# Which engine subtracts which weight remainders in an expert loop: gate+up halves on VectorE, down weights on GpSimd

## What is computed

```python
def expert_step(acc, inp):
    wg, wu, wd, c = inp
    hid = jax.nn.silu(t @ wg) * (t @ wu)
    return acc + c[:, None].astype(t.dtype) * (hid @ wd), None
```

## Time and profile before

| What | Value |
|---|---|
| median of 3 runs | 521.92 us (520.37 to 522.99) |
| profiled execution, its own time | 524.47 us |
| its span, first to last instruction | 522.7 us |
| PE busy | 458.4 us (88%) |
| DVE busy | 351.4 us (67%) |
| ACT busy | 257.7 us (49%) |
| POOL busy | 155.1 us (30%) |
| L574, remainders of a on POOL, 128 x 1024 | 32 in all, about 2.6 us each in the page's mean |
| L1288, remainders of c on DVE, 128 x 1024 | 32, mean 1630 ns |
| L1282, remainders of b on DVE, 128 x 1024 | 30, mean about 1210 ns |

### The profile page before, as it was taken

The page is one execution under the profiler, slowest core; times in us unless marked ns, Lnnn a source line. Parts: engine busy times, 40 slices in busy tenths (PEclk is TensorE's granted clock), DMA queues, the critical chain, the costliest instruction groups (busy, mean ns, idle before and its releaser), DMA issues.

```text
span 522.7 us, 7094 instructions
## 1 busy us (share of the span) xinstructions
PE 458.4 (88%) x2819; PEld 396.8 (76%) x2819; DVE 351.4 (67%) x506; ACT 257.7 (49%) x382; POOL 155.1 (30%) x104
## 2 busy tenths in 40 slices
PE   2799999999999899995999985899999999999500
PEld 2378888899898899995999975777877877877400
DVE  3414688755677969797733457368788788788357
ACT  5615283424453242226211361278888888887412
POOL 3510000000000000202100042477887887885100
PEclk9799999999999899998999997899999999999955
DMA  7532222240202222060496044269999999982175
GB/s 285 223 141 66 96 81 81 80 144 19 81 0 81 82 81 81 0 242 1 128 399 242 5 164 158 84 234 351 341 359 378 360 369 366 356 307 112 29 281 222
DMA packets 20496, 92.96 MB, mean 178 GB/s; under 512 B 6204, under 2 KB 6248, under 8 KB 12008
## 3 DMA queue, kind: packets, MB, share of 16 engines
q1 hardware_dynamic: 15784, 81.94, 42.4%
q0 software_dynamic: 4096, 8.40, 4.9%
q10 hardware_dynamic: 576, 2.10, 1.0%
HBM read 87.18 MB, written 11.53 MB: 189 GB/s over the span
## 4 chain that ended last, share of the span: by engine, by line
PE 63%; DVE 18%; ACT 8%; DMA 4%; issue 3%; POOL 1%; SPq 0%; POOLq 0%; DVEq 0%
PE bank L1385 44%; DVE actl L1288 6%; ACT acth L836 3%; ACT acth L820 2%; PE bank L1638 2%; PE bank L1640 2%; PE bank L1639 2%; PE bank L1626 2%; DMA X<-in_x_dram 2%; DVE arena L1342 1%; PE bank L1528 1%; PE bank L1544 1%; DMA arena<-pairs_dram 1%; PE bank L1666 1%; PE bank L1392 1%
## 5 line engine op out<-in xcount | busy, mean ns | idle before, releaser
L1385 PE MATMUL bank<-wh,acth 128*128 128x256 f32 x320 | 92.9, 290 | 1.4 <-DVE arena L951 1.4
L1385 PE MATMUL bank<-wh,actl 128*128 128x256 f32 x320 | 91.9, 287 | 0.0
L1385 PE MATMUL bank<-wl,acth 128*128 128x256 f32 x320 | 91.8, 287 | 0.0
L574 POOL TENSOR_TENSOR wl<-raw,wh 128x1024 fp32r<-128x1024 f32 x22 | 57.0, 2611 | 70.9 <-ACT wh L809 70.9
L537 POOL TENSOR_TENSOR arena<-arena,bc 128x1024 f32<-128x1024 f32 x2 | 5.3, 2670 | 206.6 <-DVE arena L963 206.6
L1385 PEld LDWEIGHTS bank<-wh,acth 128*128 128x128 f32 x320 | 63.1, 197 | 1.6 <-issue 1.6
L1385 PEld LDWEIGHTS bank<-wl,acth 128*128 128x128 f32 x320 | 62.8, 196 | 0.0
L1385 PEld LDWEIGHTS bank<-wh,actl 128*128 128x128 f32 x320 | 62.7, 196 | 0.0
L1288 DVE TENSOR_TENSOR actl<-arena,acth 128x1024 fp32r<-128x1024 f32 x32 | 52.1, 1630 | 2.7 <-ACT acth L820 1.0
L1638 PE MATMUL bank<-wh,acth 128*128 128x512 f32 x128 | 53.4, 417 | 0.5 <-DVE actl L1274 0.3
L1385 PE MATMUL bank<-acth,wh 128*128 128x512 f32 x128 | 50.5, 394 | 0.0
(11 more groups left out here) (287 smaller groups left out, 998.5 us busy)
## 6 DMA issues: line engine op xcount, KB each, us to landing
raw<-in_w_units_dram SPq DMA_DIRECT2D x18, 1024.0 KB, 4.8
raw<-in_w_gate_up_dram SPq DMA_DIRECT2D x17, 1024.0 KB, 11.3
arena<-in_w_down_dram SPq DMA_DIRECT2D x16, 1024.0 KB, 13.9
arena<-in_w_gate_up_dram SPq DMA_DIRECT2D x15, 1024.0 KB, 13.0
arena<-pairs_dram SPq DMA_DIRECT2D x8, 512.0 KB, 7.3
X<-in_x_dram SPq DMA_DIRECT2D x4, 512.0 KB, 6.0
arena<-in_x_dram SPq DMA_DIRECT2D x1, 2048.0 KB, 9.7
h_dram<-X ACTq DMA_DIRECT2D x4, 512.0 KB, 3.5
```

What stands on the lines that cost most here:

```text
L574: gp.tensor_tensor(wl[:, 0, c], raw_a[b][:, c], wh[:, 0, c].bitcast(F32), ALU.subtract).then_inc(wla_ok, 1)
L1385: ins = te.matmul(acc_ap, a, b, start=(j == 0), stop=(j == n - 1))
```

## The change

The three subtractions keep their sizes, types and number. DVE takes a and b, POOL takes c. On DVE the a half stands behind b and ahead of the evacuation of the result, and for expert 1 it stands ahead of the loop. On POOL c of expert e+1 stands behind the gather and ahead of the scatter of e. Ahead of the loop POOL subtracts b and then c of expert 0 (a and then b before), and DVE subtracts a of expert 0 after the tables (c before).

```diff
-            def split_a(step, e):
+            def split_c(step, e):
                 b = e % WSETS
                 for h in range(2):
                     c = slice(h * UNIT // 2, (h + 1) * UNIT // 2)
-                    pool.wait_ge(wha_ok, step * 2 + (h + 1))
-                    gp.tensor_tensor(wl[:, 0, c], raw_a[b][:, c], wh[:, 0, c].bitcast(F32),
-                                     ALU.subtract).then_inc(wla_ok, 1)
+                    pool.wait_ge(whc_ok, step * 2 + (h + 1))
+                    gp.tensor_tensor(wcl[:, c], raw_c[b][:, c], wch[:, c].bitcast(F32),
+                                     ALU.subtract).then_inc(wlc_ok, 1)
...
                 if not first_round:
-                    split_a(base, 0)
-                split_a(base + 1, 1)
+                    split_c(base, 0)
                 for e in range(NE):
-                    if e + 2 < NE:
-                        split_a(base + e + 2, e + 2)
                     if e + HGB < NE:
                         gather(base, e + HGB, first_round)
+                    if e + 1 < NE:
+                        split_c(base + e + 1, e + 1)
                     scatter(r, base, e)
 
-            split_a(0, 0)
             for h in range(2):
...
+            split_c(0, 0)
...
-            def split_c(step, e, h):
-                c = slice(h * UNIT // 2, (h + 1) * UNIT // 2)
-                dve.wait_ge(whc_ok, step * 2 + (h + 1))
-                ve.tensor_tensor(wcl[:, c], raw_c[e % WSETS][:, c], wch[:, c].bitcast(F32),
-                                 ALU.subtract).then_inc(wlc_ok, 1)
+            def split_a(step, e):
+                for h in range(2):
+                    c = slice(h * UNIT // 2, (h + 1) * UNIT // 2)
+                    dve.wait_ge(wha_ok, step * 2 + (h + 1))
+                    ve.tensor_tensor(wl[:, 0, c], raw_a[e % WSETS][:, c], wh[:, 0, c].bitcast(F32),
+                                     ALU.subtract).then_inc(wla_ok, 1)
 
             def dve_expert(r, base, e, first_round):
                 step, b = base + e, e % 2
                 if e + 1 < NE:
                     rest_tokens(step + 1, 1 - b)
-                if e:
-                    split_c(step, e, 0)
                 dve.wait_ge(sil_ok, step + 1)
                 ve.tensor_tensor(hid, bank[b][:, FE:2 * FE], sil, ALU.mult).then_inc(hid_ok, 1)
-                if e:
-                    split_c(step, e, 1)
                 dve.wait_ge(hh_ok, step + 1)
                 ve.tensor_tensor(hidl[:, :], bank[4][:, 0:FE], hidh[:, :].bitcast(F32), ALU.subtract).then_inc(hl_ok, 1)
                 if e + 1 < NE:
                     split_b(step + 1, e + 1)
+                if e + 2 < NE:
+                    split_a(step + 2, e + 2)
...
-                split_c(base, 0, 0)
-                split_c(base, 0, 1)
+                split_a(base, 0)
                 if not first_round:
                     split_b(base, 0)
                 rest_tokens(base, 0)
+                split_a(base + 1, 1)
```

## The result

The changed kernel takes 538.36 us (median of 4, 537.32 to 539.66), the one before 522.33 in the same comparison. The ratio is 1.0307 with a 95% interval of 1.0278 to 1.0337: **16.0 us slower**, where 13.2 were forecast. The profiled execution took 539.66 us, and its span is 537.9. T stands for the end of the down product of the expert before.

A forecast was written before the change was run, and what follows sets the result against it. PE's own work was taken to bound the loop, with a stall of about 0.35 us an expert on top. Loop 10.0, last expert 0.8, expert 0 0.6 and routing 1.8 made +13.2: 535.1 us at the median, range 530 to 548.

The forecast's parts named there:

- What bounds the kernel now: Expert loop before the change: PE's own work, plus hid queued behind VectorE's held c half, about 0.35 us an expert.
- The loop: Experts 1 to 14: the down product waits about 0.9 for GpSimd's c; period 10.46 us, +10.0 us in all.
- Covers: In the loop, VectorE's late token remainders cost PE no wait or 0.1 to 0.5, hidden under its wait for c.
- the rival in which they starve: Loop: gather and scatter wait out VectorE's four subtractions, delaying GpSimd's next pair; +12.5, 547.6 us, chance 0.14.
- The routing: Ahead of the loop: VectorE's small operation L1218 meets GpSimd's fourth half; +1.8 us, bounds 0 and 2.3.
- The early loads: Expert 3's a and b loads leave with the gathers and may delay the second one; bounds 0 and +0.7, taken as 0.
- VectorE's order: Expert 0: VectorE subtracts a of expert 1 ahead of expert 1's token remainders, delaying PE's first a half; +0.6 us.
- The last expert: Its down product waits for GpSimd's c, starts at T+5.99 and ends at T+9.06 instead of T+8.24; +0.8 us.

The follow-up runs named there:

- the old order: Changed kernel, but ahead of the loop GpSimd again subtracts a and b of expert 0 and VectorE c; 533.68 us, ratio to before 1.0254.
- half of c: Changed kernel, but GpSimd's pair subtracts only the first 512 columns of each half of c; 518.77 us, ratio to before 0.9939.
- shared c: Changed kernel, but in the loop GpSimd subtracts the first half of c and VectorE the second; 530.49 us, ratio to before 1.0141.
- down product by halves: Changed kernel, but PE runs both output banks with c's first half, then its second, waiting for each half alone; 529.54 us, ratio to before 1.0140.
- 8 and 16 matmuls: Changed kernel plus 8 or 16 matmuls into a free bank in the last expert's idle stretch of PE; 537.98 us with 8, 539.0 with 16.

## Why the prediction was right, and where it was short

- **What bounds the kernel now: right.** The stall of `hid` behind the held c half was put at 0.35 us an expert and 4 to 5 us in all. With half of a left out on GpSimd 14 experts took 131.69 instead of 136.43.
- **The loop: right.** Forecast 10.46 an expert from ACT's start of c, the pair of 4.75 and a down product of 3.07; measured 10.49. The order of the causes is shown as well: with the pair short the period is 9.41, and with the pair off PE's path VectorE's chain sets 9.89, a little less than the 10.05 that follows from the chain's 6.8.
- **Covers: right.** The token remainders were said to come up to 0.5 late under PE's wait for c. With that cover gone PE waited for them up to 0.7 (its weight loads up to 1.1), in every second expert. Gather and scatter got in between VectorE's subtractions and were done at T+11.6 (11.7 forecast), so the rival in which they starve did not come.
- **The routing: right.** +1.7 against +1.8. L1217, the fourth small operation with two inputs, took 2.26 where its like had 0.17, and it went away with the old order.
- **The early loads: the term of the sum that was mis-sized.** I bounded it at 0.7 from the landing time of a gather in the loop, 9.7, and took 0 because the loads begin with the gathers. They begin behind the second gather's issue, and it landed 10.75 after it in the changed kernel, 1.05 later than the bound had it. PE also asked for it at 337.21 and not at 337.85, so it waited 2.4, and it lost clock. The price is 2.0 in that profile (23.57 less 21.56). VectorE's order took 0.4 beside it (0.6 forecast). The bound was a median under load, and what counted was one transfer with 2 MB issued right behind it.
- **The last expert: +2.3 in the profile against +0.8.** The start of its down product, T+5.96, was forecast at T+5.99: the wait was right. The down product then ran 4.59 instead of 3.07 at a clock that had fallen. The clock was not in the sum, but the table above has the same fall without the change's longer wait, so these 1.5 are not shown to come from the change. The mean effect of the change on it is open, and by the medians it is small.

So the 2.8 us between forecast and result are the second gather for the most part: 2.0 by the profiles, 2.9 by the medians, 1.3 by the ratios. The loop added another 0.5, with 10.49 an expert for the 10.46 of the forecast.

## What to carry to other kernels

Before handing a step to the slower engine, ask how much lead its operand has. a could be rounded and subtracted two experts ahead, and its pair on GpSimd cost 0.34 us an expert, and that only through VectorE's wait. c can't be touched before the last down product is over, so on GpSimd all that its pair takes beyond some 3.8 us (an estimate, from the prediction's sum) stands on the path. Add up what two engines need of a resource that they take in turns: here GpSimd's pair (4.75) and VectorE's four (4.7) fill 9.45 of a period of 9.41 to 9.8. Both assignments of whole units that were measured, a or c on GpSimd, paid a wait somewhere (b on GpSimd was not run). What gained was a finer cut, half of c, with a consumer that takes operands as they come; the finer cut alone did not. And a step that releases a landing buffer also times a load: moving it can put 2 MB in front of a transfer that someone waits for.

## What the runs showed that I had not expected

- The first gathers landed 5.2 us after issue (median of four) where no load left beside them, and the second one 10.75 after its issue where two 1 MB loads were issued 0.9 and 1.3 us behind it. The same order ahead of the loop stood in six profiled kernels (changed, half of c, shared c, down product by halves, 8 and 16 matmuls), and expert 0 ended 22.7 to 26.2 after the first gather's start in them: the delay is not a fixed price.
- Profiles with the same idle stretch of 1.83 us in PE had a granted clock of 0.62 and of 1.00 in the down product behind it. So had two with 1.03 us (0.63 and 1.00).
- VectorE's row of the second c half begins at 400.58, GpSimd's at 400.77 (above), and GpSimd still went first: VectorE's took 3.64 for 1.21 of work. Its operation before ended at 400.66, so a row can begin before its instruction takes its turn.
